# Gated DeltaNet recurrence: small products of norms and gates spread over a tile's period, the next tile's first inverse made at the end of this one, the inverse and its transpose in banks of their own, exponents split into two fp32r halves

## The reference, cut to what matters

```python
gc = jnp.cumsum(g, axis=-1)                       # per chunk of 64 tokens (16 for a sample)
decay = jnp.exp(jnp.where(causal, gc[..., :, None] - gc[..., None, :], NEG))
kb = k * beta
lower = jnp.where(strict, jnp.einsum("...id,...jd->...ij", kb, k) * decay, 0.0)
rhs = jnp.concatenate([v * beta, kb * jnp.exp(gc)[..., None]], -1)
sol = lax.linalg.triangular_solve(lower + jnp.eye(chunk), rhs, left_side=True, lower=True, unit_diagonal=True)
u, w = sol[..., :dv], sol[..., dv:]
intra = jnp.where(causal, jnp.einsum("...id,...jd->...ij", q, k) * decay, 0.0)

def step(s, inp):                                 # over the chunks, in order
    v_new = u_i - jnp.einsum("bhck,bhkv->bhcv", w_i, s)
    o = einsum(q_i * jnp.exp(gc_i), s) + einsum(a_i, v_new)
    s = s * jnp.exp(g_last) + einsum(k_i * jnp.exp(g_last - gc_i), v_new)
```

## Time and profile before

| what | value |
|---|---|
| median of 3 executions | 3621.76 us (3619.01 to 3628.89) |
| the profiled execution, own time | 3624.39 us |
| its span (first to last instruction) | 3622.9 us |
| TensorE busy, of the span | 3384.1 us (93%), 27409 instructions |
| VectorE, ScalarE, GpSimd busy | 58%, 41%, 11% |
| mean granted clock of TensorE | 0.965 |

### The profile page before, as it was taken

How to read it: one execution, slowest core, us unless ns; L and a number is a source line. 1 busy time by engine, 2 the same in 40 slices (tenths; PEclk the granted TensorE clock), 3 DMA queues, 4 the chain that set the end, 5 groups by cost and what they waited for, 6 DMA issues and landing times. The chain is left out here.

```text
span 3622.9 us, 68574 instructions
## 1 busy us (share of the span) xinstructions
PE 3384.1 (93%) x27409; PEld 3026.2 (84%) x27409; DVE 2093.3 (58%) x3522; ACT 1470.3 (41%) x2803; POOL 407.5 (11%) x603
## 2 busy tenths in 40 slices
PE   7999999976899996999698699999999999999997
PEld 7999999944788885666587699999899899899995
DVE  2655556654344443666488465565565565575695
ACT  1334444443244443666343343343343343343353
POOL 0000000021344442000133000000000000000000
PEclk9999999987999998999899799999999999999999
DMA  7577666742011104433376645455454455454464
GB/s 223 168 228 225 202 187 185 199 133 65 20 38 36 36 27 148 132 123 106 123 221 203 188 138 151 126 174 150 129 171 150 128 171 152 126 167 144 143 192 130
DMA packets 706409, 521.52 MB, mean 144 GB/s; under 512 B 64648, under 2 KB 650615, under 8 KB 706043
## 3 DMA queue, kind: packets, MB, share of 16 engines
q1 hardware_dynamic: 658312, 427.16, 40.4%
q0 software_dynamic: 26576, 70.12, 5.6%
q10 hardware_dynamic: 21216, 19.93, 1.8%
HBM read 432.11 MB, written 86.05 MB: 143 GB/s over the span
## 5 line engine op out<-in xcount | busy, mean ns | idle before, releaser
L1219 PE MATMUL ps_gate_up<-h2T_group_high,w_gate_up_high 128*128 128x384 f32 (+1 forms) x2112 | 689.0, 326 | 23.2 <-DVE w_gate_up_low L1315 16.8
L1220 PE MATMUL ps_gate_up<-h2T_group_low,w_gate_up_high 128*128 128x384 f32 (+1 forms) x2112 | 688.0, 326 | 0.0
L1221 PE MATMUL ps_gate_up<-h2T_group_high,w_gate_up_low 128*128 128x384 f32 (+1 forms) x2112 | 688.0, 326 | 0.0
L1219 PEld LDWEIGHTS ps_gate_up<-h2T_group_high,w_gate_up_high 128*128 128x128 f32 x2112 | 398.4, 189 | 25.9 <-issue 25.9
L1220 PEld LDWEIGHTS ps_gate_up<-h2T_group_low,w_gate_up_high 128*128 128x128 f32 x2112 | 398.4, 189 | 0.0
L1221 PEld LDWEIGHTS ps_gate_up<-h2T_group_high,w_gate_up_low 128*128 128x128 f32 x2112 | 398.3, 189 | 0.0
L1315 DVE TENSOR_TENSOR w_gate_up_low<-w_gate_up,w_gate_up_high 128x1024 fp32r<-128x1024 f32 x264 | 322.3, 1222 | 62.3 <-ACT w_gate_up_high L1253 51.6
L1321 DVE TENSOR_TENSOR w_down_low<-w_down_ring,w_down_high 128x512 fp32r<-128x512 f32 x264 | 182.4, 693 | 290.5 <-ACT w_down_high L1259 290.3
L1253 ACT ACTIVATE w_gate_up_high<-w_gate_up 128x1024 fp32r<-128x1024 f32 x264 | 279.1, 1057 | 163.0 <-PE ps_gate_up L1221 137.1
L1259 ACT ACTIVATE w_down_high<-w_down_ring 128x512 fp32r<-128x512 f32 x264 | 166.0, 631 | 331.3 <-PE ps_down L1231 170.9
L433 PE MATMUL ps_feature<-hT_high,w_in_high 128*128 128x384 f32 (+1 forms) x816 | 271.8, 333 | 9.5 <-DVE hT_low L607 8.4
(11 more groups left out here) (435 smaller groups left out, 6698.9 us busy)
## 6 DMA issues: line engine op xcount, KB each, us to landing
w_gate_up<-in_w_gate SPq DMA_DIRECT2D x132, 512.0 KB, 3.7
w_gate_up<-in_w_up SPq DMA_DIRECT2D x132, 512.0 KB, 3.7
w_down_ring<-in_w_down SPq DMA_DIRECT2D x264, 256.0 KB, 2.8
w_in_ring<-in_w_in SPq DMA_DIRECT2D x84, 512.0 KB, 4.2
w_ada_ring<-in_w_ada SPq DMA_DIRECT2D x48, 512.0 KB, 5.2
s_ck_rows<-in_cache_c_k SPq DMA_DIRECT2D x32, 512.0 KB, 7.0
s_cv_rows<-in_cache_c_v SPq DMA_DIRECT2D x32, 512.0 KB, 5.3
d_convT<-scratch_convT SPq DMA_DIRECT2D x17, 576.0 KB, 4.3
```

The costliest lines, as they stand in the source:

```text
L1219: pe.matmul(out, w_high, h_high, start=(k == 0), stop=False)
L1220: pe.matmul(out, w_high, h_low, start=False, stop=False)
L1221: last = pe.matmul(out, w_low, h_high, start=False, stop=(k == DC - 1))
```

## The change

- `norms_and_sums` is taken apart into `norms(n, heads)` and `gate_sums(n)`. The gate sums of tile k+2 stand behind the fourth addition, its norms in three parts of two heads: ahead of products(k+1, 0), behind the last addition, and behind the first inverse. They write into spare columns of `ps_Y`, not `ps_P`. VectorE's copy of the gate sums is a step of its own (`sums_copied`).
- The first inverse of tile k+1 is made at the end of iteration k. TensorE makes the inverse alone; its transpose is X_1 itself, which ScalarE copies into the second bank (`inverse_begun`); for tile 0 TensorE makes both.
- The inverse stands in one bank, copied by VectorE, the transpose in the other, copied by ScalarE. Products wait for the first alone, additions for the second.
- The two rows of factor logarithms that go onto diagonals are split: ScalarE rounds them to fp32r (`rows_rounded`), VectorE subtracts the rounded from the full row, GpSimd makes diagonals of both (eight multiplications), and `exponents` adds two fp32r products in place of one f32 product.
- into_state(k-1, 1) moves from behind the fourth addition to behind the level 5 product, products(k+1, 1) ahead of that product.
- At the start SyncE waits for tile 0 before it loads tile 1, and the clearing of the three operands stands behind the second tile's gate sums on VectorE.

```diff
-        diag = sb("d_log_diag", [P, H, 2, C])
+        row_high, row_low = sb_r("d_row_logs_high", [P, 2, H]), sb("d_row_logs_low", [P, 2, H])
+        diag_high, diag_low = (sb_r(f"d_log_diag_{n}", [P, H, 2, C]) for n in ("high", "low"))
+        seq_sum_r = sb_r("d_seq_sum", [P, P])
...
-        small = ps_P[:, W:]
+        small = ps_Y[:, W:]
...
             load(0)
+            sp.wait_ge(loaded[0], 32)
             load(1)
...
+                pool.wait_ge(s["rows_split"], n + 1)
                 if n:
                     pool.wait_ge(s["G_done"], 2 * n)
                 for half in range(2):
-                    for a, f in enumerate((QG, KBE)):
-                        row = fac_log[:, f].rearrange("p (j a) -> p a j", a=2)[:, half]
-                        last = pool.tensor_tensor(diag[:, halves[half], a, :], ident[:].unsqueeze(1).to_broadcast([P, J, C]),
-                                                  row.unsqueeze(2).to_broadcast([P, J, C]), ALU.mult)
+                    for diag, rows in ((diag_high, row_high[:].bitcast(F32)), (diag_low, row_low[:])):
+                        for a in range(2):
+                            row = rows[:, a].rearrange("p (j a) -> p a j", a=2)[:, half]
+                            last = pool.tensor_tensor(diag[:, halves[half], a, :], ident[:].unsqueeze(1).to_broadcast([P, J, C]),
+                                                      row.unsqueeze(2).to_broadcast([P, J, C]), ALU.mult)
                 last.then_inc(s["diag_ready"], 1)
...
+            def norms(n, heads):
+                if 0 in heads:
+                    pe.wait_ge(s["squares_ready"], n + 1)
+                else:
+                    pe.wait_ge(s["sums_ready"], n + 1)
+                for f in heads:
                     last = pe.matmul(small[:, SS + 2 * f:SS + 2 * f + 2], squares[:, f, :], in_seq[:, 0, 0:2],
                                      start=True, stop=True)
-                last.then_inc(s["norms_done"], 1)
+                if H - 1 in heads:
+                    last.then_inc(s["norms_done"], 1)
+
+            def gate_sums(n):
                 kind, seqs = int(sample(n)), seqs_of(n)
                 pe.wait_ge(s["g_ready"], n + 1)
+                if n:
+                    pe.wait_ge(s["logs_ready"], n)
...
-                pe.matmul(ps_P[:, 0:W], seq_sum[:, 0, :], flat(diag[:, halves[half]]), start=True, stop=True)
+                pe.matmul(ps_P[:, 0:W], seq_sum_r[:], flat(diag_high[:, halves[half]]), start=True, stop=False)
+                pe.matmul(ps_P[:, 0:W], seq_sum_r[:], flat(diag_low[:, halves[half]]), start=False, stop=True)
...
+                if n:
+                    pe.wait_ge(s["X_ready0"], Y_base(n))
+                quadrants(ps_X[:, 0], lambda r, i: X_1[r, i, :], lambda r, i: K["ident"][r, r], True).then_inc(s["Z_done0"], 1)
+                if n == 0:
+                    quadrants(ps_X[:, 1], lambda r, i: K["ident"][r, r], lambda r, i: X_1[r, i, :], True)
...
+                pe.wait_ge(s["X_ready0"], Y_base(n) + l)
+                if l == 1:
+                    pe.wait_ge(s["logs_ready"], min(n + 2, TILES))
+                    pe.wait_ge(s["sums_ready"], min(n + 2, TILES))
+                if l == 5:
+                    pe.wait_ge(s["sums_ready"], min(n + 3, TILES))
+                quadrants(ps_Y, lambda r, i: L[r, l, i, :], lambda r, i: X[r, i, :], True).then_inc(s["Y_done"], 1)
...
+                turned = X_1 if l == 1 else X_T
                 pe.wait_ge(s["Y_ready"], Y_base(n) + l)
-                for half in range(2):
-                    if l < last_level(n):
-                        quadrants(inverse_at(0), lambda r, i: X[r, i, 1, :], lambda r, i: Y[r, i, :], heads_of(half), False, True)
-                    quadrants(inverse_at(1), lambda r, i: Y[r, i, :], lambda r, i: X[r, i, 1, :], heads_of(half), False, True
-                              ).then_inc(s[f"Z_done{half}"], 1)
+                if l == 1:
+                    if n:
+                        pe.wait_ge(s["base_ready"], n)
+                else:
+                    pe.wait_ge(s["X_ready1"], Y_base(n) + l - 1)
+                if l < last_level(n):
+                    quadrants(ps_X[:, 0], lambda r, i: turned[r, i, :], lambda r, i: Y[r, i, :], False).then_inc(s["Z_done0"], 1)
+                quadrants(ps_X[:, 1], lambda r, i: Y[r, i, :], lambda r, i: turned[r, i, :], False).then_inc(s["Z_done1"], 1)
...
+                if exists(k + 2):
+                    norms(k + 2, range(0, 2))
...
                     add_to_inverse(k, 4)
+                if k == 1:
+                    sample_into_state(4)
+                if exists(k + 2):
+                    gate_sums(k + 2)
+                if preparing:
+                    products(k + 1, 1)
+
+                if 5 in inverting:
+                    lower_times_inverse(k, 5)
                 if solving:
                     into_state(k - 1, 1)
-                if k == 1:
-                    sample_into_state(4)
-                if preparing:
-                    products(k + 1, 1)
-
-                if 5 in inverting:
-                    lower_times_inverse(k, 5)
-                if exists(k + 2):
-                    norms_and_sums(k + 2)
                 if k == 1:
                     sample_into_state(5)
                 if 5 in inverting:
...
                 if k == 1:
                     sample_into_state(6)
                     sample_into_state(7)
+                if exists(k + 2):
+                    norms(k + 2, range(2, 4))
+                if exists(k + 1):
+                    first_inverse(k + 1)
+                if exists(k + 2):
+                    norms(k + 2, range(4, H))
                 if exists(k - 2):
                     turn_out(k - 2)
...
+            def rows_rounded(n):
+                act.wait_ge(s["fac_log_ready"], n + 1)
+                act.activation(row_high[:], fac_log[:, QG:KBE + 1], ACT.Identity).then_inc(s["row_high_ready"], 1)
+
+            def inverse_begun(n):
+                act.wait_ge(s["X_1_ready"], n + 1)
+                act.wait_ge(s["X_ready1"], Y_base(n))
+                act.activation(ps_X[:, 1, 0:W], X_1[:].rearrange("p h c -> p (h c)"), ACT.Identity).then_inc(s["base_ready"], 1)
+
             def inverse_copied(n, l):
-                act.wait_ge(s["Z_done1"], X_base(n) + l + 1)
-                if l < last_level(n):
-                    last = act.activation(flat(X[:, halves[1]]), ps_X[:, 1, 0:W], ACT.Identity)
-                else:
-                    last = act.activation(XT[:, halves[1]], ps_X[:, 1, 0:W].rearrange("p (h a c) -> p h a c", a=2, c=C)[:, :, 1],
-                                          ACT.Identity)
-                last.then_inc(s["X_ready1"], 1)
+                act.wait_ge(s["Z_done1"], Y_base(n) + l)
+                dst = X_T if l < last_level(n) else XT
+                act.activation(dst[:].rearrange("p h c -> p (h c)"), ps_X[:, 1, 0:W], ACT.Identity).then_inc(s["X_ready1"], 1)
...
                     product_copied(k, 5)
+                if 5 in inverting:
+                    inverse_copied(k, 5)
+                if exists(k + 1):
+                    inverse_begun(k + 1)
                 if exists(k + 2):
                     norm_logs(k + 2)
-                if 5 in inverting:
-                    inverse_copied(k, 5)
                 if exists(k - 2):
                     mix_copied(k - 2)
...
+            def sums_copied(n):
+                seqs = seqs_of(n)
+                dve.drain()
+                if n:
+                    dve.wait_ge(s["fac_ready"], n)
+                dve.wait_ge(s["sums_done"], n + 1)
+                dve.tensor_copy(sums[:, 0:2 * H + seqs * J], small[:, GC:GC + 2 * H + seqs * J]).then_inc(s["sums_ready"], 1)
...
+                dve.wait_ge(s["row_high_ready"], n + 1)
+                dve.tensor_tensor(row_low[:], fac_log[:, QG:KBE + 1], row_high[:].bitcast(F32), ALU.subtract
+                                  ).then_inc(s["rows_split"], 1)
...
             decays(1)
+            sums_copied(1)
+            for t in (s_state, s_wT, s_qT):
+                last = dve.memset(t[:], 0.0)
+            last.then_inc(s["blank_ready"], 1)
...
                     sample_state_updated(4)
+                if exists(k + 2):
+                    sums_copied(k + 2)
                 if preparing:
                     matrices(k + 1, 1)
-                if 5 in inverting:
-                    inverse_copied(k, 5)
+                if solving:
+                    state_updated(k - 1, 1)
```

88 lines of the change are left out of this document (28 added, 60 removed).

## The result

The changed kernel takes 3604.70 us (median of 5, 3598.69 to 3606.95), the kernel before 3621.93 (5, 3619.01 to 3628.89): a ratio of 0.9949, 95% interval 0.9938 to 0.9960. The profiled execution of the changed kernel took 3604.70 with a span of 3603.2. It was forecast at 3604.

A forecast was written before the change was run, and what follows sets the result against it. TensorE's queue was taken to set the steady pace. Thirteen periods at -1.7 us (-22), tiles 1, 2 and last (-0.5, -0.5, -1.0) and start +6 gave -18; 3624.4 - 18 - 2.6 = 3604 us, range 3588 to 3622.

The forecast's parts named there:

- The clock: Thirteen prompt periods: splitting the 2.06 us block of small products ends the clock falls; period 28.19 to 26.5 us.
- Rival 1: Steady periods: the clock falls as often as now, at new light stretches; 15 us not won, 3619 us; chance 0.20.
- Norms and sums, +0.3: TensorE's norms and gate sums: unchanged work, but three more matmul-size round trips; +0.3 us a tile (0 to 0.5).
- First inverse, -0.70: TensorE's first inverse: half of its 48 records go, two groups of 0.35; -0.70 us a tile.
- wait ahead of the first level's product, -0.22 + 0.1: Before the first level's product: the wait for VectorE's copy goes (-0.22), one for the norms' logarithms comes (+0.1 us).
- Exponents, -0.70: Exponent products at levels 3 and 4: two fp32r matmuls replace two f32 records; 0.30 plus 0.40 us saved a tile.
- The level-2 wait, +0.7: Second level's product: TensorE waits for VectorE's inverse copy, queued behind logarithms and a subtraction held by GpSimd masks; +0.7 us.
- Rival 2: Second level's product: no wait there; saves 10 us over the stage, 3593 us; chance 0.15.
- rival 3: Second level: factor logarithms catch one mask later, wait 1.7 us a tile, and the clock falls there; 3634 us; chance 0.12.
- The start, +6: Stage start: later memsets delay tile 2's loads, then GpSimd's diagonals and tile 1's exponents by 12 us; half returns, +6.
- Rival 4: Stage start: loses twice as much, because the late loads hold more than tile 1; 3612 us; chance 0.05.

The follow-up runs named there:

- one_block: The changed kernel with the norms of all six heads and the gate sums in one block again behind the fourth addition: 3634.7 us.
- copy_first: The changed kernel with VectorE's copy of the first level's inverse queued ahead of the factor logarithms instead of behind them: 3598.3 us.
- gaps_and_copy: The changed kernel with three memsets in VectorE's idle stretches and its copy of the first level's inverse ahead of the factor logarithms: 3587.0 us.

## Why the prediction was right

The case forecast came true, in its mechanisms too: the clock no longer falls, the level-2 wait came, and the start lost time by the chain that was named. That the time came out within 1 us is luck all the same. The start cost 4.9 us more than forecast, and the rest of the stage gave 5.8 more (2.9 in the thirteen periods, 0.8 ahead of them and 2.1 behind; the last two were not taken apart).

**The clock.** Right, and shown from both sides: no fall in the changed kernel, nine with the block put back. Rival 1 (3619) is out.

**Norms and sums, +0.3.** The three parts of the norms take 0.54, 0.47 and 0.54, so 1.55 for 1.33: +0.2, and one_block says 0.12 to 0.16.

**First inverse, -0.70; wait ahead of the first level's product, -0.22 + 0.1.** Its 24 records take 0.84 (1132.28 to 1133.12), where 48 took 1.45: -0.6. The -0.12 of the wait did not come: from turn_out's start to the product it is 0.70 (1133.59 to 1134.29), and before it was 0.47 and the 0.22. The profile names nothing that ends the 0.18 left of the wait; in the program the product waits there for the logarithms of the norms.

**Two pieces that the sum put at nothing.** They are found when the full-clock period before is laid beside a changed one piece by piece. Timeline before, ScalarE's copy of the second bank and two rows of TensorE:

```profile
1141.79 0.49 ACT L2925 ACTIVATE d_inverse<-ps_d_inverse 128x384 f32<-128x384 f32 x1 [1.06 <-PE ps_d_inverse L2631]
...
1143.78 0.52 PE L2631 MATMUL ps_d_inverse<-d_LX,d_inverse 64*64 64x64 f32 x12
...
1160.54 0.93 PE L2766 MATMUL ps_d_update<-d_v_new,d_k_decay 64*128 64x128 f32 x6
```

Timeline of TensorE, changed kernel, the period shown above:

```profile
1127.84 0.76 PE L2690 MATMUL ps_d_prepared<-d_convT 64*64 64x128 f32 x10
...
1136.06 0.90 PE L2634 MATMUL ps_d_inverse<-d_LX,d_inverse_first 64*64 64x64 f32 x24
```

From the first level's product to its addition it was 1.99 (1141.79 to 1143.78) and is 1.77 (1134.29 to 1136.06). Before, the second half of that product waited inside it: its thirteenth record starts at 1142.33, 0.19 behind the twelfth, when ScalarE's copy ends (1142.28). The prediction saw that product wait for VectorE's copy only. And products(k+1, 1), the fifth level's product, into_state and the last addition take 3.90 in the new order (1127.84 to 1131.74) instead of 4.09 (1160.54 to 1163.78, and 1165.84 to 1166.69). So -0.2 each; into_state's move was not tried by itself.

**Exponents, -0.70.** The two fp32r products and the mask product take 0.73 up to the addition, one f32 product with its mask 1.01: -0.28 at level 3 and about as much at level 4, -0.55 in all. The 0.30 credited at level 3 held; the 0.40 at level 4 did not, because 0.17 a product is what they take in a row and the first of a pair, entered from the 64-row products, takes 0.25 to 0.28.

Timeline of TensorE, one exponent product in the changed kernel:

```profile
1145.80 0.44 PE L2679 MATMUL ps_d_prepared<-d_log_diag_high,d_seq_sum 128*128 128x384 f32 x1
1146.08 0.34 PE L2680 MATMUL ps_d_prepared<-d_log_diag_low,d_seq_sum 128*128 128x384 f32 x1
1146.26 0.34 PE L2681 MATMUL ps_d_prepared<-d_expo_mask_half,d_ident_half 128*128 128x384 bf16 x1
1146.53 0.68 PE L2634 MATMUL ps_d_inverse<-d_LX,d_inverse_turning 64*64 64x64 f32 x16
```

**The level-2 wait, +0.7.** It came, at the place and for the engines named, and is 0.55 on average; copy_first takes it away whole. Its detail was wrong. I held the subtraction by the fourth mask; it takes 0.17 behind the masks, and it is the four operations ahead of it that are held, one mask each. The Trainium skill's page SBUF — State Buffer, "Who interferes with whom", has a VectorE instruction with two SBUF inputs blocked by a GpSimd instruction that reads SBUF. The trace agrees for the three of the four that have two inputs there (0.88 to 1.04 beside 0.17), and the rule said nothing false of the subtraction, which met no long pass. The first of the four, a TENSOR_SCALAR with one input, lasted 1.05 beside its mask all the same. Rival 2 (no wait) is out; rival 3's late mask exists, in the two periods with a gap of 1.59, but no clock fall follows it.

The pieces as measured make +0.2 - 0.6 - 0.2 - 0.2 - 0.55 + 0.55 = -0.8; the period fell by 0.77 against the full-clock tile. Against 28.19 it is 1.92 shorter where 1.7 was forecast: -24.9 for -22.

**The start, +6.** Mechanism right (memsets: up to 14.5 us, GpSimd's queue: 5.5), size +10.9. Tile 2's rows were expected on GpSimd 52.9 us behind the stage's begin (917) and came at 52.8; a gain that I had not counted (2.2 us, the first rows) went against a slower landing. Two things failed. The diagonals were to take 4.2 us from there and took 7.3: one pair of 0.98 lasted 4.09, beside VectorE's product of the sample state. The same section of the Trainium skill says that whichever engine is first gets the shared ports and the other is blocked. The trace agrees: VectorE's product is in work from 913.82, the second product of that pair starts behind it, at 914.24, and here it is GpSimd that waits, a direction that my count did not look at.

The other is what comes back behind the exponents: 3.6 us for 5.6, and by other pieces than I had counted. Timeline of that stretch before, with VectorE's product of the sample state:

```profile
913.08 3.34 DVE L3119 TENSOR_TENSOR d_s_faded<-d_s_state,d_decay 128x3072 f32<-128x3072 f32 x1
...
917.03 1.62 PE L2676 MATMUL ps_d_prepared<-d_log_diag,delta_seq_sum 128*128 128x384 f32 x2 [4.47 <-DVE d_matrices L3096]
...
922.31 2.69 PE L2646 MATMUL ps_d_prepared<-delta_in_seq,d_squares 128*128 128x2 f32 x12 [0.82 <-DVE d_matrices L3096]
```

Timeline of TensorE in the changed kernel, gate sums and second norms of tile 2:

```profile
926.02 0.43 PE L2654 MATMUL ps_d_LX<-d_g,delta_run_sum 128*128 128x6 f32 x2
...
928.68 1.01 PE L2644 MATMUL ps_d_LX<-delta_in_seq,d_squares 128*128 128x2 f32 x4
```

I let the norms and sums drop out of it, 4 us at the half clock. They took 3.8 (922.31 to 926.11), but four of the six heads' norms and the gate sums still stand there in the new order, some 3.1 us in three places. What went instead is most of the 4.47 that TensorE waited there for VectorE, since the product of the sample state is now done ahead of it (0.82 is left). And 1.99 of a new wait came, for the first inverse's input from GpSimd; I had put that at nothing as long as later matmuls cover it, and 2 without; behind tile 0, which has three levels, the covering matmuls of level 5 do not exist.

Rival 4's start (twice the loss, 12) came nearly to size, from other causes than its own; its 3612, which is 3610 by the terms of the sum, fails by the 6 us that the rest of the stage gave on top.

## What to carry to other kernels

A block of small products can cost as much again through the clock behind it as by itself (1.15 to 2.2 us a tile beside its own 2.1 here); taking it apart cost 0.1 to 0.2. When an edit queues more small VectorE work ahead of a copy that TensorE needs, put the copy first: here it also removed a wait that differed from period to period and from run to run. Count the start of a stage by its queues: what is moved off an idle front may stand, two queues further, ahead of everything that the second tile needs.

## What was not expected of the hardware

- GpSimd can be the one that waits: two products of 128x192 took 4.09 us beside a 128x3072 VectorE product with two SBUF inputs, 0.98 without it. In gaps_and_copy a GpSimd copy of 128x48 took 3.36 beside the same product, 0.22 without it.
- VectorE operations with one SBUF input were held by GpSimd's passes too: a TENSOR_SCALAR of 128x6 took 1.05 us beside a mask, 0.16 without one (gaps_and_copy).
- The level-2 gap takes steps more than a spread: mostly 0.42, 0.83, 1.15 or 1.58 us, by which mask VectorE's chain gets past. Programs that differ only at the start had none or four periods of 1.58, 3 us over the stage.
- The second load, issued 1.07 us behind the first, made the small rows of other queues land 2.3 us later (ScalarE's first operation at 8.1 us of the stage instead of 5.8).
